# Both norms of a layer boundary from sums gathered during the output tiles, their factors held in columns, and GpSimd adding the last block's new input rows

## The reference, cut to what matters

```python
def rms_norm(x, g):
    y = xf * lax.rsqrt(jnp.mean(xf * xf, axis=-1, keepdims=True) + EPS)
    return (y * g.astype(jnp.float32)).astype(x.dtype)
for l in range(DEPTH):                                   # DEPTH = 2
    h  = rms_norm(x,  norm_pre[l]) * (1.0 + sc[:, None]) + sh[:, None]
    hc = rms_norm(xc, norm_pre[l]) * (1.0 + scc) + shc
    ...                                                  # z = h @ w_in[l], three branches
    out = merge_branches(z, (y_a, y_b, y_c), w_branch[l], w_out[l])
    x_new = x + gt[:, None] * rms_norm(out, norm_post[l])
    ...                                                  # the same for xc, where l is 0
# second block: h = rms_norm_2(x, g_mix), then its projections
```

## Time and profile before

| what | us |
|---|---|
| median of 3 runs | 1451.06 |
| lowest, highest | 1448.44, 1453.69 |
| span of the profiled execution (no other time of it is printed) | 1448.2 |
| busy in it: PE, PEld | 1391.8 (96%), 1176.7 (81%) |
| busy in it: DVE, ACT, POOL | 923.0 (64%), 689.0 (48%), 41.8 (3%) |

### The profile page before, as it was taken

How to read it: one execution, slowest core, us unless ns; L and a number is a source line. 1 busy time by engine, 2 the same in 40 slices (tenths; PEclk the granted TensorE clock), 3 DMA queues, 4 the chain that set the end, 5 groups by cost and what they waited for, 6 DMA issues and landing times.

```text
span 1448.2 us, 20966 instructions
## 1 busy us (share of the span) xinstructions
PE 1391.8 (96%) x8380; PEld 1176.7 (81%) x8380; DVE 923.0 (64%) x1625; ACT 689.0 (48%) x1190; POOL 41.8 (3%) x50
## 2 busy tenths in 40 slices
PE   5999999999999999989999999988999999999998
PEld 2577668777888888669888899987988999888888
DVE  5555764776523444388775777657667777888546
ACT  5333544234322232555356454455556746666444
POOL 0000000000000000100000000010000002000001
PEclk9999999999999999999999999998999999999999
DMA  9321343144332232623234455554543345655552
GB/s 369 134 89 58 145 160 117 44 154 161 104 113 87 87 102 75 226 70 99 77 119 143 137 177 190 184 166 126 183 145 112 95 145 176 200 188 194 191 174 74
DMA packets 57794, 202.36 MB, mean 140 GB/s; under 512 B 6272, under 2 KB 9536, under 8 KB 57696
## 3 DMA queue, kind: packets, MB, share of 16 engines
q1 hardware_dynamic: 55568, 194.01, 40.3%
q0 software_dynamic: 1760, 6.25, 1.3%
q10 hardware_dynamic: 368, 0.74, 0.2%
HBM read 199.93 MB, written 1.05 MB: 139 GB/s over the span
## 4 chain that ended last, share of the span: by engine, by line
PE 88%; DVE 8%; ACT 3%; DMA 1%; issue 1%; ACTq 0%; DVEq 0%; SPq 0%
PE gemm_bank L415 17%; PE gemm_bank L417 16%; PE gemm_bank L416 16%; PE misc_bank L415 4%; PE misc_bank L416 4%; PE misc_bank L417 4%; PE misc_bank L426 3%; PE gemm_bank L426 3%; PE gemm_bank L571 1%; PE misc_bank L571 1%; PE misc_bank L427 1%; PE gemm_bank L427 1%; PE misc_bank L823 1%; PE gemm_bank L504 1%; PE misc_bank L864 1%; DVE wlo L1729 1%
## 5 line engine op out<-in xcount | busy, mean ns | idle before, releaser
L1729 DVE TENSOR_TENSOR wlo<-raw,whi 128x1024 fp32r<-128x1024 f32 x316 | 382.8, 1223 | 75.5 <-ACT whi L1208 71.9
L1208 ACT ACTIVATE whi<-raw 128x1024 fp32r<-128x1024 f32 x316 | 332.7, 1055 | 168.9 <-PE gemm_bank L417 101.5
L415 PE MATMUL gemm_bank<-halves,wlo 128*128 128x256 f32 (+1 forms) x1152 | 375.3, 326 | 19.1 <-DVE halves L2192 5.9
L417 PE MATMUL gemm_bank<-halves,whi 128*128 128x256 f32 (+1 forms) x1152 | 360.1, 313 | 0.0
L416 PE MATMUL gemm_bank<-halves,whi 128*128 128x256 f32 (+1 forms) x1152 | 360.0, 312 | 0.0
L415 PEld LDWEIGHTS gemm_bank<-halves,wlo 128*128 128x128 f32 x1152 | 222.5, 193 | 43.4 <-issue 18.8
L417 PEld LDWEIGHTS gemm_bank<-halves,whi 128*128 128x128 f32 x1152 | 222.8, 193 | 12.1
L416 PEld LDWEIGHTS gemm_bank<-halves,whi 128*128 128x128 f32 x1152 | 223.2, 194 | 11.2 <-issue 0.7
L415 PE MATMUL gemm_bank<-arena_r,wlo 128*128 128x512 f32 (+1 forms) x320 | 108.3, 338 | 0.5 <-DVE wlo L1729 0.5
L417 PE MATMUL gemm_bank<-arena_r,whi 128*128 128x512 f32 (+1 forms) x320 | 107.6, 336 | 0.0
L416 PE MATMUL gemm_bank<-arena_r,whi 128*128 128x512 f32 (+1 forms) x320 | 107.6, 336 | 0.0
(11 more groups left out here) (419 smaller groups left out, 2289.4 us busy)
## 6 DMA issues: line engine op xcount, KB each, us to landing
raw<-in_stream SPq DMA_DIRECT2D x348, 512.0 KB, 3.4
arena<-in_stream SPq DMA_DIRECT2D x16, 512.0 KB, 11.3
x<-in_x SPq DMA_DIRECT2D x1, 1024.0 KB, 6.3
x<-in_ctx SPq DMA_DIRECT2D x1, 1024.0 KB, 9.8
y<-in_hy_decay POOLq DMA_DIRECT2D x2, 512.0 KB, 4.5
arena<-in_gm_ws POOLq DMA_DIRECT2D x2, 512.0 KB, 5.4
const_b<-in_const_b POOLq DMA_DIRECT2D x1, 763.0 KB, 6.6
y<-in_hy_w POOLq DMA_DIRECT2D x2, 256.0 KB, 4.0
```

What stands on the lines that cost most here:

```text
L415: mm(out, w_lo, r_hi, start=first, stop=False)
L417: return mm(out, w_hi, r_hi, start=False, stop=last)
L1208: act.activation(self.whi[:, t % SPLIT, :], self.raw_tile(t), ACT.Copy).then_inc(*self.mark("tile_hi", "tile_hi", t))
L1729: dve.tensor_tensor(self.wlo[:, t % SPLIT, :], self.raw_tile(t), self.whi[:, t % SPLIT, :].bitcast(F32), ALU.subtract).then_inc(*self.mark ...
```

## The change

During the output tiles two more sums are gathered. ACT adds per tile and half a square of the gated result (b²) and does the gated result first. DVE adds b·x per tile and a running sum of it. POOL adds up both squares, two instructions per tile. The sums of x² come from four more matmuls at the program's front. In place of the sums with 512 or 256 columns PE multiplies 128-token slices with one column of 1/1024 (N=1: the result is one column per 128 tokens), so the norms' factors are 128x2 columns, on which DVE and ACT do their small operations (`dve_cols`, `dve_energy`, `dve_norm_new`, `act_norm_out`, `act_norm_new`). Two 128x128 matmuls per factor spread it over all partitions again (`pe_norm_spread`). The rows then need no sum of their own: per row DVE makes the scaled b, the sum for h, x_new and the low part, interleaved over k.

At the first boundary ACT's evictions of the query results and its row work are in another order, the keys come side 0 first, and the second half of the filter's spectrum is made after the keys. At the second boundary POOL adds the rows of the new `x`, and PE does `zc0`, `zc1`, `head0`, `head1` by the table `QUAD` (`pe_last_quad`), then `head2`.

```diff
-CROSS_KEYS = ((0, 0), (1, 0), (2, 0), (0, 1), (1, 1), (3, 0), (2, 1), (3, 1))
+CROSS_KEYS = ((0, 0), (1, 0), (2, 0), (3, 0), (0, 1), (1, 1), (2, 1), (3, 1))
...
-POOLED = (("out", 0), ("out", 1), "g_ffn")
+POOLED = ("g_ffn",)
...
+    def norm_sums(self, s):
+        return self.sq_sum[:, self.half(s)], self.piece(7, s), self.piece(6, s)
+    def norm_last(self, s):
+        return self.tmp[:, (KT - 1) % 2, self.half(s)], self.piece(5, s), self.piece(3, s)
...
+    def pe_norm_sums(self, l, s):
+        pe, (bank, c) = self.pe, self.norm_bank(s)
+        pe.wait_ge(*self.at("pooled", ("out", l), KT - 2))
+        pe.wait_ge(*self.at("xb_sum", l, KT - 2))
+        for a, src in enumerate(self.norm_sums(s)):
+            for e in range(2):
+                pe.matmul(bank[:, c + 4 * a + 2 * e:c + 4 * a + 2 * e + 1], src[:, e * P:(e + 1) * P], self.c["mean_all"][:, 0:1], start=True, stop=True)
...
+    def pe_norm_spread(self, l, s, i):
+        pe = self.pe
+        pe.wait_ge(*self.at("norm_r", l, s, i))
+        if s:
+            pe.wait_ge(*self.at("h", l + 1, 0, KT - 1))
+        for e in range(2):
+            r = self.norm_r[:, 4 * s + 2 * i + e:4 * s + 2 * i + e + 1]
+            m = pe.matmul(self.spread_bank(i)[:, e * P:(e + 1) * P], r.broadcast_to([P, P]), self.ident, start=True, stop=True)
+        m.then_inc(*self.mark("pe_norm", "spread_r", l, s, i))
...
-            if step in CROSS_SUMS:
-                self.pe_cross_sum(1, CROSS_SUMS.index(step))
+            if step == 2 * KT + 7:
+                for r in range(2):
+                    self.pe_norm_spread(0, 1, r)
...
-        for k in range(KT):
-            self.pe_cross_sum(0, k)
+        self.pe_norm_last(0, 0)
+        self.pe_norm_sums(0, 1)
+        self.pe_norm_spread(0, 0, 0)
+        self.pe_norm_last(0, 1)
+        self.pe_norm_spread(0, 0, 1)
+        self.pe_spec(1, 0, 1)
         self.pe_cross_queries(queries)
         for i, side in CROSS_KEYS:
             self.pe_cross_keys(keys[i], side, (i, side) == (0, 1))
+        self.pe_spec(1, 1, 2)
         self.pe_next += 8
...
+    def pe_last_quad(self):
+        pe, n = self.pe, 0
+        tiles = self.tiles[self.pe_next:self.pe_next + 4]
+        for i, k in QUAD:
+            T = tiles[i]
+            s, c = T.t % SPLIT, slice(k * P, (k + 1) * P)
+            if k == 0:
+                pe.wait_ge(*self.at("tile_lo", T.t))
+                self.pe_bank(T.use)
+            if k == n:
+                pe.wait_ge(*self.at("hn", "g_mix", k))
+                n += 1
...
         pe.wait_ge(*self.landed("cv_w2"))
-        pe.wait_ge(*self.at("rstd", ("res", 1)))
-        self.pe_tiles(2)
-        self.pe_heads(3)
+        self.pe_last_quad()
+        self.pe_tiles(1)
+        for n in range(2):
+            self.pe_head(n)
         self.pe_tiles(4)
...
-            self.act_sq(("out", l), j, n, b[:, 0:n]).then_inc(*self.mark("act_sq", "sq", ("out", l), j))
-            for s in range(n // TOK):
-                t = slice(s * TOK, (s + 1) * TOK)
-                m = act.activation(self.branch_out(j, s), b[:, t], ACT.Identity, bias=self.c["zero"], scale=self.mods[l][:, 16 + j, s:s + 1])
-            m.then_inc(*self.mark("act_evac", "evac", T.use))
+            if j >= 2:
+                act.wait_ge(*self.at("pooled", ("out", l), max(1, j - 2)))
+            gate = [self.mods[l][:, 16 + j, s:s + 1] for s in range(n // TOK)]
+            for s, g in enumerate(gate):
+                act.activation(self.branch_out(j, s), b[:, self.half(s)], ACT.Identity, bias=self.c["zero"], scale=g).then_inc(*self.mark("act_branch", "branch", l, j, s))
+            act.activation(self.tmp[:, j % 2, 0:n], b[:, 0:n], ACT.Square).then_inc(*self.mark("act_sq", "sq", ("out", l), j))
+            for s, g in enumerate(gate):
+                m = act.activation(self.piece(2 + j % 2, s), b[:, self.half(s)], ACT.Square, scale=g)
+                m.then_inc(*(self.mark("act_sq", "bsq", l, j, s) if s < n // TOK - 1 else self.mark("act_evac", "evac", T.use)))
+            self.also("bsq", l, j, n // TOK - 1)
...
     def act_cross(self):
         act = self.act
-        act.wait_ge(*self.at("summed", ("out", 0), KT - 1))
-        for s in range(2):
-            self.act_cross_root(("out", 0), s)
+        self.act_norm_out(0, 0)
+        self.act_hi()
+        self.act_norm_new(0, 0)
+        self.act_norm_out(0, 1)
         self.act_tap_root(1)
-        self.act_hi()
-        for k in range(KT):
-            self.act_cross_sq(0, k)
-            if k in (3, 5):
-                self.act_kern(1, (k - 3) // 2)
-        act.wait_ge(*self.at("summed", ("res", 0, 0), KT - 1))
-        self.act_cross_root(("res", 0), 0)
         act.wait_ge(*self.at("mod", 1))
-        self.act_cross_h(0)
+        self.act_cross_h(0, 0, 2)
+        self.act_kern(1, 0)
+        self.act_cross_h(0, 2, 5)
+        self.act_norm_new(0, 1)
+        self.act_cross_h(0, 5, KT)
         for i in range(4):
-            for k in CROSS_SQ[i]:
-                self.act_cross_sq(1, k)
-            self.act_tiles(1)
-        act.wait_ge(*self.at("summed", ("res", 0, 1), KT - 1))
-        self.act_cross_root(("res", 0), 1)
-        self.act_cross_h(1)
+            self.act_hi()
+            self.act_cross_h(1, i, i + 1)
+        self.act_tiles(4, split=False)
+        self.act_cross_h(1, 4, KT)
...
+        self.act_hi()
+        self.act_tiles(2, split=False)
         act.activation(self.mask[:, 0:P], self.ident, ACT.Copy, scale=0.0)
         act.activation(self.mask[:, P:2 * P], self.c["causal"], ACT.Copy).then_inc(*self.mark("act_half", "mask"))
-        self.act_tiles(2)
...
+                dve.wait_ge(*self.at("xb_sum", l, j - 1))
+            if j < KT - 1:
+                dve.wait_ge(*self.at("branch", l, j, n // TOK - 1))
+                self.own(dve.tensor_tensor(to, self.both_halves(j, 0, n), self.by_half(self.x[:, j, 0:n], n), ALU.mult))
+                if j:
+                    dve.tensor_tensor(acc, acc, to, ALU.add).then_inc(*self.mark("dve_norm", "xb_sum", l, j))
+            else:
+                for s in range(n // TOK):
+                    dve.wait_ge(*self.at("branch", l, j, s))
+                    dve.tensor_tensor(self.piece(5, s), self.branch_out(j, s), self.x[:, j, self.half(s)], ALU.mult).then_inc(*self.mark("dve_norm", "xb", l, j, s))
...
+        v.wait_ge(*self.at("root_out", l, s))
+        v.reciprocal(r, r).then_inc(*self.mark("dve_norm", "norm_r", l, s, 0))
+        v.wait_ge(*self.at("norm_r", l, s, 0))
+        self.own(v.tensor_tensor(t, cols[:, 4:6], r, ALU.mult))
+        self.own(v.scalar_tensor_tensor(t, cols[:, 2:4], 2.0, t, ALU.mult, ALU.add))
+        self.own(v.tensor_tensor(t, t, r, ALU.mult))
+        for c in range(2):
+            m = v.tensor_scalar(e[:, c:c + 1], t[:, c:c + 1], e[:, c:c + 1], EPS, ALU.add, ALU.max)
+        m.then_inc(*self.mark("dve_norm", "energy", l, s))
...
+    def dve_cross_rows(self, s):
+        v = self.dve
+        v.wait_ge(*self.at("spread_r", 0, s, 0))
+        for k in range(KT + 2):
             if k < KT:
-                v.scalar_tensor_tensor(self.tmp[:, (0, 1, 3, 4)[k % 4], c], self.x[:, k, c], self.modA[:, k, s:s + 1], self.tmp[:, 2, c], ALU.mult, ALU.mult).then_inc(*self.mark("dve_h", "h_sum", 1, s, k))
-            if s == 0 and k == 3:
+                self.dve_scaled(0, s, k)
+            if s == 0 and k == 1:
+                self.dve_cols(0, 1)
+            if k == 1:
+                v.wait_ge(*self.at("spread_r", 0, s, 1))
+            if 1 <= k <= KT:
+                self.dve_cross_sum(s, k - 1)
+            if k < KT:
+                self.dve_new(0, s, k)
+            if k >= 2:
+                self.dve_cross_lo(s, k - 2)
+            if s == 0 and k in (3, 5):
+                (self.dve_energy if k == 3 else self.dve_norm_new)(0, 1)
+            if s == 0 and k == 6:
+                self.dve_tap_rs(1)
+            if s == 0 and k == 2 or s and k in (0, 1, 2, 3):
                 self.dve_lo()
-            if k:
-                q = k - 1
-                v.wait_ge(*self.at("h_hi", 1, s, q))
-                v.scalar_tensor_tensor(self.lo(q, s), self.tmp[:, (0, 1, 3, 4)[q % 4], c], mod[:, q, s:s + 1], self.hi(q, s).bitcast(F32), ALU.add, ALU.subtract).then_inc(*self.mark("dve_half", "h", 1, s, q))
     def dve_cross(self):
         self.dve_lo()
-        self.dve_cross_rstd(("out", 0), 0)
-        self.dve_tap_rs(1)
-        for k in range(KT):
-            self.dve_cross_new(0, k)
-        self.dve_cross_rstd(("out", 0), 1)
-        self.dve_cross_rstd(("res", 0), 0)
+        self.dve_cols(0, 0)
+        self.dve_energy(0, 0)
+        self.dve_norm_new(0, 0)
         self.dve.wait_ge(*self.at("mod", 1))
-        self.dve_cross_h(0)
-        for k in range(KT):
-            self.dve_cross_new(1, k)
-        for _ in range(4):
-            self.dve_lo()
-        self.dve_cross_rstd(("res", 0), 1)
-        self.dve_cross_h(1)
-        self.dve_kern(1)
```

(32 more changed lines are left out.)

183 lines of the change are left out of this document (116 added, 67 removed).

## The result

The changed kernel takes 1491.68 us (median of 4 runs, 1488.40 to 1498.97) against 1450.38 us: a ratio of 1.0295 (95% interval 1.0264 to 1.0325), so it is slower by about 41 us. The forecast had the sign right and the size wrong: 1476, with 1487 as its upper end. The profiled execution is the longest of the four (1498.97), a span of 1497.7 against 1448.2.

A forecast was written before the change was run, and what follows sets the result against it. TensorE, busy 96% of the span, was taken as the bound, with gains only in two 16 us gaps. First boundary 16.9, front 1.0 and second boundary 8.0 sum to +25.9: 1476 us forecast, range 1461 to 1487.

The forecast's parts named there:

- Output tiles: the step that failed: Layer 0's output tiles: added product and sum counted only as DVE backlog at the end, 3.6 us, before the tap sums.
- the table's second row: First to last output product of layer 0: forecast change 0, from 54.7 us in before.
- Up to h: First boundary, last output tile to first complete h: 642.4 against 644.65, so 2.3 us earlier.
- Six single columns take 1.4 at most: First boundary, PE's columns between the tap sums and DVE's reduction: 1.4 us at most, ending at 635.9.
- Pause ahead of the keys: First boundary, last query to first key product: PE idle 11 to 12 us; deciding term, +16.9 up to the value tiles.
- turns: First boundary, ACT and DVE alternating key-tile parts with rows of half 1 ahead of the keys: 3.6 us a turn.
- spectrum and value tile: Behind the keys: two spectrum products, 1.8 us, then ACT's copy and the first value tile's parts, up to 702.4.
- Layer 1: Value tiles to the last output product of layer 1: forecast change 0.
- Second boundary: Last output product of layer 1 to the long stall's end: +8 us (bounds +4 and +10); quad start +4.4.
- The rivals: Whole kernel, beside the low clock: overlapping turns, 1470 or 1467, chance 0.15; faster, 1445, 0.05; no change, 1451, 0.04.
- The low clock: Rival: low clock stays through the queries and the keys' start, adding 5 to 9: 1482 to 1486, chance 0.16.
- The rule on the shared port: Second boundary's rows: full DVE stops by POOL's additions would cost 5.3 us more; the prediction took shared delay instead.

The follow-up runs named there:

- go with the order: Changed kernel with the low part of the next output tile made ahead of the product b*x and its sum in layer 0's output tiles: 1482.32 us, ratio 1.0214.
- Moving the transfers: Changed kernel with POOL's four transfers at the second boundary issued ahead of its eight row additions: 1485.74 us, ratio 1.0249.
- The best full version, with DVE's rows: Changed kernel with four orders put right, and DVE instead of POOL adding the rows of new x at the second boundary: 1460.12 us, ratio 1.0084.
- The small products moved away: DVE's-rows version with PE's small products moved behind query steps and half 1's columns read after half 0's last row: 1465.05 us, ratio 1.0114.

## Why the prediction was wrong

- *Output tiles: the step that failed.* "DVE carries as backlog four operations ... which it has to do before the tap sums are ready" took the added product and sum as a backlog at the end, and the table's second row as nothing, without a reason given. But in four places two modulation tiles stand between one output tile and the next, which need no low part and take PE about 1 us together. There the low part of the next output tile comes directly behind the product of the tile just finished: a loop from PE over ACT and DVE back to PE. The row is +12 us in the runs with the same code here (66.7 against 54.7), and 10.5 of them go with the order (56.2). Added alone to before, product and sum cost 13.5 in this stretch (54.7 to 68.2).
- *Up to h: mis-sized.* Forecast 13.8 us after the last output tile, found 19.9 after the start of its last product (16.4 in before): h comes later, not 2.3 earlier. "Six single columns take 1.4 at most": they took 2.56, since 12 passes at 0.21 are the price at the low clock, and half 1's columns stand in PE's order ahead of each of half 0's two spreads, which start 1.7 and 3.6 us after their factors are there (657.34 and 660.75). DVE's part was met by POOL's addition too, a product of 0.69 took 1.76.
- *Pause ahead of the keys: right.* 10.83 against 11 to 12, released by the eviction, turns 3.5 against 3.6; keys with their low clock 25.9 against 26.2; spectrum and value tile 4.6 against 4.9.
- *Layer 1: missed, 3.7.* Before, the value tiles ran at a clock of 1.00, after the pause of 2.89 at 0.86 over 22 us, which is 3.1. The other 0.7 are its own output tiles, and go with POOL's additions. Without the pause it is no better (289.4 to 290.8): then the waits for DVE in the attention stand in its place. The prediction follows the spectrum's second half up to the value tiles alone.
- *Second boundary: right.* +6.7 against +8. The quad starts 5.6 us later than in before (forecast 4.4), after a wait of 13.35; the rows came 1.4 us apart (forecast 1.16). Moving the transfers brings back 6.6.
- *The rivals.* The low clock was given 0.16 and stands in four of the stretches above (0.90, 0.61, 0.88, 0.86), but not through the queries (0.93 from 664.4 to 680.6). In the output tiles it goes with the waits: it is 1.00 when the order is put right. Ahead of the keys and the value tiles PE stood still for 10.83 and 2.89 us. Behind the last output tile short waits and small products stand together, and no run separates them. The rule on the shared port held better than I made it: low parts of rows went from 0.42 to 0.77. Its price, though, was at the places where POOL's last sum meets DVE's last product, not 5.3 in the rows: there both versions take the same.

No version was found that beats before. Why the design itself gains nothing, the runs show in part. The best full version, with DVE's rows, has a profile 10.4 us longer than before: 1.6 in layer 0's output tiles, 5.7 from there to the value tiles, 4.2 in layer 1, nothing at the second boundary (34.5 against 34.6), 1.0 less in front and end together. Of the 5.7, 3.2 are more busy time of PE (its granted clock there is 0.86 against 0.94, and it has more small products), the rest idle time. The 4.2 are idle time of PE: it is busy for 280.0 us against 279.8. The small products moved away bring the first query product 2.5 us closer to the last output product than in before (13.9 against 16.4), but h(7) at 23.7 instead of 22.8, since DVE has four operations per row in either kernel, and the low clock then lies on the queries.

## What to carry to other kernels

Idle time of an engine covers an added instruction only if nothing that another engine waits for stands behind it: look in the order for what follows the new instruction, at every place in a loop, above all where some turns have a different shape. A sum that is gathered early moves work from a gap into a stretch that was full. When a stall is gone after an edit, compare the next stretch too: it may have come back there. And when the first item of a row of eight comes earlier, ask when the last comes, and at which clock the engine then works.

## What the runs showed of the hardware

Single-column products are not free: 0.12 us a pass at the full clock (8 took 0.95) and 0.21 at the low one (12 took 2.56). A DVE operation of 0.42 us beside a POOL addition of 0.73 took 0.77, one of 0.69 beside an addition that takes 1.3 alone took 1.76, and a low part of 1.22 up to 2.28. The Trainium skill's page "SBUF — State Buffer" (section "SBUF: two separate sides") has the port that both share as an exclusive lock, on which the later one waits. These rows agree with it.
